# Three pooling chunks move from the input projection into the even attention; a low-rank chunk in stacked parts

## What is computed

```python
# layer 0 (even)
h = rms_norm(x, norm_mix_w[0])
u, q, k, v = split(h @ w_in)                 # 512 | 512 | 128 | 128 columns
# pooling: 4 groups of 128 channels, trailing windows 2/4/8/16
total = csum[:, base:base + l, lo:hi] - csum[:, base - w:base - w + l, lo:hi]
diff = total / count - ext[:, POOL_STATE:, lo:hi]
outs.append(einsum('blc,cd->bld', diff, w_pool[g]))
ya = concatenate(outs) * scale
yb = sliding_window_attention(rope(q), rope(k), v, sinks)   # 8 heads on 2 KV heads, own chunk + 2 before
x = x + concatenate([ya, yb]) @ w_out
x = x + conv_ffn(rms_norm(x, norm_ffn_w[0]))
# layer 1 (odd): the input projection has, among others, a low-rank part of 16 columns
cq, ck, cv, cg, cr, dq, dk, dvv = split(h @ w_in)
log_a = log_sigmoid(cr @ w_gate2 + b_gate) / GATE_NORM      # forget gate of the linear attention
```

## Time and profile before

| | us |
|---|---|
| median of three runs | 1280.73 |
| the profiled execution | 1279.63 |
| its span, first to last instruction | 1277.5 |
| even layer: input projection | about 10 to 81 |
| even attention with output chunks | 81 to 154 |
| even second output pass | 154 to 178 |
| odd layer: input projection begins | 577 |

### The profile page before, as it was taken

The page is one execution under the profiler, slowest core; times in us unless marked ns, Lnnn a source line. Parts: engine busy times, 40 slices in busy tenths (PEclk is TensorE's granted clock), DMA queues, the critical chain, the costliest instruction groups (busy, mean ns, idle before and its releaser), DMA issues.

```text
span 1277.5 us, 24157 instructions
## 1 busy us (share of the span) xinstructions
PE 1223.4 (96%) x9325; PEld 1178.8 (92%) x9325; DVE 807.4 (63%) x1206; ACT 261.8 (20%) x514; POOL 699.6 (55%) x565
## 2 busy tenths in 40 slices
PE   6978899999999999999999998899999999999995
PEld 6967799999999999999999986799999999999995
DVE  6987577778787731126534688766777777762222
ACT  3015332111111200002111165422111111110002
POOL 6732257655665666665653441256665566566661
PEclk9989999999999999999999999999999999999998
DMA  5311123222222223223222310132222222222221
GB/s 212 116 58 34 32 71 100 82 82 96 85 82 86 94 83 100 99 94 115 84 83 67 102 50 33 34 110 85 97 82 82 89 92 82 83 98 93 90 81 71
DMA packets 35522, 108.88 MB, mean 85 GB/s; under 512 B 5984, under 2 KB 7792, under 8 KB 35472
## 3 DMA queue, kind: packets, MB, share of 16 engines
q1 hardware_dynamic: 29232, 102.51, 24.0%
q10 hardware_dynamic: 6240, 5.64, 1.4%
HBM read 103.00 MB, written 5.13 MB: 85 GB/s over the span
## 4 chain that ended last, share of the span: by engine, by line
PE 87%; DVE 9%; ACT 2%; issue 1%; DMA 0%; POOL 0%; ACTq 0%; POOLq 0%; SPq 0%; DVEq 0%
PE psum L424 21%; PE psum L426 20%; PE psum L425 20%; PE psum L437 6%; PE psum L435 4%; PE psum L436 4%; PE psum L438 4%; PE psum L439 3%; DVE even_winsum L1358 1%; PE psum L754 1%; PE psum L621 1%; DVE small L1579 1%; DVE even_rope_swapped L1340 1%; ACT diff_probs L1091 0%; DVE even_diff L1361 0%
## 5 line engine op out<-in xcount | busy, mean ns | idle before, releaser
L424 PE MATMUL psum<-h_hi,w_hi 128*128 128x272 f32 x2032 | 593.7, 292 | 14.4 <-DVE h_lo L1190 10.3
L426 PE MATMUL psum<-h_hi,w_lo 128*128 128x272 f32 x2032 | 588.8, 290 | 0.0
L425 PE MATMUL psum<-h_lo,w_hi 128*128 128x272 f32 x2032 | 585.8, 288 | 0.0
L395 POOL TENSOR_TENSOR w_lo<-w_raw,w_hi 128x1024 fp32r<-128x1024 f32 x187 | 465.1, 2487 | 15.6
L424 PEld LDWEIGHTS psum<-h_hi,w_hi 128*128 128x128 f32 x2032 | 383.2, 189 | 19.6 <-issue 16.7
L425 PEld LDWEIGHTS psum<-h_lo,w_hi 128*128 128x128 f32 x2032 | 383.9, 189 | 0.2
L426 PEld LDWEIGHTS psum<-h_hi,w_lo 128*128 128x128 f32 x2032 | 383.1, 189 | 0.0
L392 POOL TENSOR_TENSOR tick<-tick 1x1 f32<-1x1 f32 x183 | 38.5, 210 | 523.7 <-PE psum L426 444.4
L393 POOL TENSOR_SCALAR w_hi<-w_raw 128x1024 fp32r<-128x1024 f32 x187 | 197.5, 1056 | 9.3 <-DMA w_raw<-in_weights 8.0
L437 PE MATMUL psum<-y_both,w_hi 128*128 128x480 f32 x352 | 133.4, 379 | 0.0
L1290 DVE TENSOR_TENSOR x<-x,psum 128x240 f32 (+1 forms) x16 | 6.4, 401 | 176.1 <-PE psum L439 176.0
(11 more groups left out here) (217 smaller groups left out, 1456.1 us busy)
## 6 DMA issues: line engine op xcount, KB each, us to landing
w_raw<-in_weights SPq DMA_DIRECT2D x187, 512.0 KB, 3.5
x<-in_x SPq DMA_DIRECT2D x8, 272.0 KB, 5.6
out_y<-x SPq DMA_DIRECT2D x8, 272.0 KB, 2.4
out_diff_v_new<-odd_dv ACTq DMA_DIRECT2D x1, 1024.0 KB, 6.2
out_diff_k_new<-odd_kT ACTq DMA_DIRECT2D x1, 1024.0 KB, 4.7
even_rope<-in_rope ACTq DMA_DIRECT2D x1, 544.0 KB, 3.9
odd_rope<-in_rope ACTq DMA_DIRECT2D x1, 544.0 KB, 3.6
consts<-in_consts ACTq DMA_DIRECT2D x1, 384.5 KB, 4.7
```

The source lines that it names most:

```text
L395: pool.tensor_tensor(w_lo[:, k], w_raw[:, k % RAW], w_hi[:, k].bitcast(F32), ALU.subtract).then_inc(w_ready, 1)
L424: pe.matmul(out, wh, xh[:, cols], start=first and n == 0, stop=False)
L425: pe.matmul(out, wh, xl[:, cols], start=False, stop=False)
L426: ins = pe.matmul(out, wl, xh[:, cols], start=False, stop=last and n == len(pairs) - 1)
```

## The change

- The input projection of the even layer has 7 chunks: v, k, two of q, pooling group 3, two of q. v is transposed after the seventh. Scores of unit 0 are issued after the sixth chunk.
- The other three pooling chunks (`pool_fill`) are cut into steps of one to eight slices and put between the parts of the attention units, by the table `EVEN_U`; they use accumulator 3 and each waits for the evacuation of the one before. Window sums and differences are cut up too (`pool_add`, `pool_diff`) and stand between DVE's attention work.
- Pooling products are made half by half in bank 5 (`pool_product`, table `EVEN_POOL`); ACT scales each half into `even_diff` and makes the high part, DVE the low part from SBUF (`pooled_low`).
- The values of all blocks go to bank 4; bank 5 is free for the products.
- Output chunks 0 and 1 are cut up in the attention by `EVEN_OUT`; chunks 2 to 7 follow it and rotate over accumulators 0, 1 (the scores' banks) and 3.
- Maxima and normalisation of a unit are one group instead of two, with the sinks negated once; ACT's small exponential is one instead of two. ACT takes the exponentials of unit u + 2 ahead of the evacuation of unit u + 1. The five DMA issues for the new k and v stand after the exponentials of unit 2.
- `out_norm` makes all eight normalised slices within the pass in both layers.
- The high part of the attention half and its low part have places of their own (`e_hi`, `e_lo`), and so have `probs` and `probsT`, since h must live through the attention.
- The low-rank chunk has its 16 columns twice, at 0 to 15 and 32 to 47; POOL copies the low weights over the second set of the high ones, and PE issues 32 matmuls of 48 output rows instead of 48 (`low_rank`). The gate weights are stacked likewise, 48 rows. DVE works the first gate half at n = 2 and the second at n = 3.

The diff, cut to its core:

```diff
+        POOL_ORDER = [3, 2, 1, 0]
+
+
+
+        EVEN_U = {(-1, 1): (1, 0, 8), (0, 0): (2, 0, 1), (0, 1): (2, 1, 3), (1, 0): (2, 3, 4), (1, 1): (2, 4, 6),
+                  (2, 0): (2, 6, 8), (2, 1): (3, 0, 1), (3, 0): (3, 1, 2), (3, 1): (3, 2, 4), (4, 0): (3, 4, 5),
+                  (4, 1): (3, 5, 7), (5, 0): (3, 7, 8)}
+        EVEN_POOL = {(1, 1): (0, 0), (2, 0): (0, 1), (3, 0): (1, 0), (3, 1): (1, 1), (5, 0): (2, 0), (5, 1): (2, 1),
+                     (6, 1): (3, 0), (7, 0): (3, 1)}
+        EVEN_OUT = {(5, 1): (0, 0, 2), (6, 1): (0, 2, 3), (8, 0): (0, 3, 4), (9, 0): (1, 0, 2), (9, 1): (1, 2, 4)}
+
+        def pooled_acc(m):
+
+            return 3 if m < 2 else (0, 1, 3)[(m - 2) % 3]
...
+            pool.wait_ge(w_ready, S_ODD_IN + 1)
+            cr = S_ODD_IN % RING
+            pool.tensor_scalar(w_hi[:, cr].rearrange("p (c m) -> p c m", c=KC)[:, :, 32:48],
+                               w_lo[:, cr].bitcast(F32).rearrange("p (c m) -> p c m", c=KC)[:, :, 0:16],
+                               1.0, 0.0, ALU.mult, ALU.add).then_inc(stacked, 1)
...
+            def low_rank(acc, s, c):
+
+                wh = w_hi[:, s % RING, c * P:c * P + 48]
+                for half in range(2):
+                    cols = slice(half * HALF, (half + 1) * HALF)
+                    out = psum[0:48, 2 * acc + half, 0:HALF]
+                    pe.matmul(out, wh, h_hi[:, c, cols], start=c == 0, stop=False)
+                    ins = pe.matmul(out, wh, h_lo[:, c, cols], start=False, stop=c == KC - 1)
+                return ins
...
-                    if n >= (2 if n_norm else 3):
+                    if n_norm and n >= 2:
                         pe.wait_ge(evac, ev0 + n - 1)
+                    if not n_norm and n == 3:
+                        pe.wait_ge(rms_ready, 1)
+                    if not n_norm and n >= 4:
+                        pe.wait_ge(evac, (1, 2, 5)[n - 4])
+                    if n_norm and n == 0:
+                        pe.wait_ge(stacked, 1)
...
+                if n == EVEN_PROJ - 2:
+                    even_scores(0)
+                if n == EVEN_PROJ - 1:
+                    pe.wait_ge(evac, 3)
...
+            def pool_fill(i, k0, k1):
+                s = EVEN_PROJ + i - 1
+                if k0 == 0:
+                    pe.wait_ge(w_ready, s + 1)
+                    pe.wait_ge(evac, EVEN_PROJ + i - 1 if i > 1 else EVEN_PROJ - 1)
+                ins = tiles(3, s, h_tiles(k0, k1), k0 == 0, k1 == KC)
+                if k1 == KC:
+                    ins.then_inc(slab_done, 1)
...
+            def pool_product(i, half):
+
+                if half == 0:
+                    pe.wait_ge(diff_ready, i + 1)
+                if i == half == 0:
+                    pe.wait_ge(in_even, 16 * NEVEN)
+                    pe.wait_ge(evac, EVEN_PROJ)
                 else:
-                    pe.wait_ge(evac, ev)
-                out_chunk(s_out + m // 2, m, 3, y_hi, y_lo, 0)
-
-
-            even_scores(0)
+                    pe.wait_ge(pool_out, 2 * i + half)
+                g = POOL_ORDER[i]
+                pe.matmul(psum[:, 5, 0:HALF], e_wpool[:, g], e_diff[:, g, half * HALF:(half + 1) * HALF],
+                          start=True, stop=True).then_inc(pool_mm, 1)
...
+            def pooled_fill(m, i0, i1):
+                s = S_EVEN_OUT + m // 2
+                if i0 == 0:
+                    pe.wait_ge(w_ready, s + 1)
+                    if m == 0:
+                        pe.wait_ge(evac, EVEN_IN)
+                    elif m == 1:
+                        pe.wait_ge(x_upd, 1)
+                    elif m >= 4:
+                        pe.wait_ge(x_upd, m - 2)
+                for i in range(i0, i1):
+                    if m == 0:
+                        pe.wait_ge(pool_lo, i + 1)
+                    c = POOL_ORDER[i]
+                    ins = tiles(pooled_acc(m), s, [(4 * (m % 2) + c, y_hi[:, c], y_lo[:, c])], i == 0, i == 3)
+                if i1 == 4:
+                    ins.then_inc(slab_done if m % 2 else mid_done, 1)
...
+            in_projection(0, 0, 0, EVEN_PROJ, even_side)
+            even_fill(-1, 1)
             even_scores(1)
-            pe.wait_ge(evac, EVEN_IN)
-            pool_product(0, 3)
             for u, (b, c) in enumerate(EU):
                 (q0, nq), _, runs = even_block(b)
-                pe.wait_ge(p_norm, 2 * u + 2)
+                pe.wait_ge(p_norm, u + 1)
                 pr = probs[u % 2][:, :].rearrange("p (h k) -> p h k", h=4)
                 for kb, (_, kn) in enumerate(runs):
                     for j in range(4):
                         ins = pe.transpose(psum[0:kn, 2 * (u % 2) + kb, j * nq:(j + 1) * nq],
                                            pr[0:nq, j, kb * P:kb * P + kn], ident[0:nq, 0:nq])
                 ins.then_inc(p_turned, 1)
-                if u in EVEN_FILL:
-                    out_fill(S_EVEN_OUT, EVEN_FILL[u], 0, EVEN_IN)
                 if u >= 1:
                     even_values(u - 1)
+                even_fill(u, 0)
                 if u + 2 < len(EU):
                     even_scores(u + 2)
+                even_fill(u, 1)
             even_values(9)
-            for m in range(len(EVEN_FILL), KC):
-                out_fill(S_EVEN_OUT, m, 0, EVEN_IN)
-            pe.wait_ge(y_lo_done, 9)
+            for m in range(2, KC):
+                pooled_fill(m, 0, 4)
...
+            ac.wait_ge(turned, 1)
+            ac.activation(e_v[:, 0:4], psum[:, 2, :].rearrange("p (t f) -> p t f", t=4), ACT.Copy)
+            ac.activation(e_v[0:SMP, 4], psum[0:SMP, 3, 0:P], ACT.Copy).then_inc(v_out, 1)
+
+            def pooled(i, half):
+
+                g = POOL_ORDER[i]
+                ac.wait_ge(pool_mm, 2 * i + half + 1)
+                ac.activation(e_diff[:, g, half * HALF:(half + 1) * HALF], psum[:, 5, 0:HALF], ACT.Copy,
+                              scale=const("pool_scale")[:, g:g + 1]).then_inc(pool_out, 1)
+                if half:
+                    ac.wait_ge(pool_out, 2 * i + 2)
+                    ac.activation(y_hi[:, g], e_diff[:, g], ACT.Copy).then_inc(pool_hi, 1)
...
             even_exp(0)
-            pooled(4, 0, 3)
+            even_turned(0)
             even_exp(1)
-            even_turned(0)
             for u, (b, c) in enumerate(EU):
-                if u + 1 < len(EU):
-                    even_turned(u + 1)
+                if u >= 1:
+                    even_turned(u)
+                if c == 0 and b >= 1:
+                    even_out(b - 1)
+                if (u, 0) in EVEN_POOL:
+                    pooled(*EVEN_POOL[u, 0])
                 if u + 2 < len(EU):
                     even_exp(u + 2)
-                if c == 1:
-                    (q0, nq), _, _ = even_block(b)
-                    ac.wait_ge(o_ready, u + 1)
-                    ac.activation(h_hi[:, 4:8, q0:q0 + nq],
-                                  psum[:, 4 + b % 2, 0:4 * nq].rearrange("p (j q) -> p j q", j=4),
-                                  ACT.Copy).then_inc(y_hi_done, 1)
+                if (u, 1) in EVEN_POOL:
+                    pooled(*EVEN_POOL[u, 1])
+                if u == 0:
+                    dma(io["swa_v_new"][0], e_v[:, 3], out_done)
+                    dma(io["swa_v_new"][1, 0:P - SMP], e_vc[SMP:P, :], out_done)
+                    dma(io["swa_v_new"][1, P - SMP:P], e_v[0:SMP, 4], out_done)
+                    ac.wait_ge(rope_done, 1)
+                    dma(io["swa_k_new"][:, 0], e_kT[:, SEQ - P:SEQ], out_done)
+                    dma(io["swa_k_new"][:, 1], e_kT[:, KEYS - P:KEYS], out_done)
+            even_out(4)
...
+            for n in range(4):
+                even_in(n)
+            pool_in(0)
             even_max(0)
+            even_in(5)
+            even_normalise(0)
+            even_in(6)
+            for i in (1, 2):
+                pool_add(3, i)
+            pool_in(1)
             even_max(1)
-            pooled_low(4, 0, 3)
-            even_normalise(0)
             for u, (b, c) in enumerate(EU):
                 if u + 1 < len(EU):
                     even_normalise(u + 1)
-                if u in EVEN_FILL:
-                    out_first(S_EVEN_OUT, EVEN_FILL[u], 0, 0)
                 if c == 0 and b >= 1:
                     even_low(b - 1)
+                if u == 2:
+                    pool_in(2)
+                if u == 5:
+                    pool_in(3)
+                if u == 7:
+                    pooled_low(2)
                 if u + 2 < len(EU):
                     even_max(u + 2)
-            for m in range(len(EVEN_FILL), KC):
-                out_first(S_EVEN_OUT, m, 0, 0)
-            even_low(4)
+                if u == 0:
+                    for i in (3, 4):
+                        pool_add(3, i)
+                    pool_diff(3)
+                if u == 1:
+                    for i in (1, 2, 3):
+                        pool_add(2, i)
+                if u == 2:
+                    pool_diff(2)
+                if u == 3:
```

(21 more changed lines are left out.)

288 lines of the change are left out of this document (129 added, 159 removed).

## The result

The changed kernel takes **1283.68 us** (median of 18 runs, 1281.66 to 1285.87), the kernel before, in runs beside it, 1280.37 us (18 runs, 1279.58 to 1282.07). The ratio is 1.0024 (95% interval 1.0017 to 1.0031): slower by 3.1 us by the ratio (3.3 by the medians), just over the 0.2% that a measurement of this kernel can tell from no change. The forecast was 1281.4 us, no change. The profiled execution spans 1281.9 us against 1277.5.

The account below looks back on a forecast made before the run. TensorE was taken as the bound, busy 1223.4 of 1277.5 us. Even part +1.6, odd part -1.0 and norms +0.1 gave +0.7 us, 1280.3 for the profiled execution and 1281.4 us as median; range 1278.5 to 1284, with rivals 1274.5 to 1287.

Parts of the forecast that it names:

- (a): Early even attention: PE waits for DVE's pooling evacuation before the third pooling chunk, with two POOL meetings; 4.1 us idle.
- (b): Before unit 3's scores: PE waits for ACT's evacuation of unit 1's transposes, behind exponentials and five DMA issues; 3.7 us idle.
- (c): Units 3 to 7 and before unit 8: ACT's order makes a 5.1 us loop between scores; 4.7 us idle.
- (d): Output chunk 0's third step waits for the third pooled remainder, behind unit 8's normalisation on DVE; 4.7 us idle.
- (e): The last two attention units of the even layer: 2.3 us idle.
- three episodes: Low clock after three long even-part stalls: 1.54 us each plus half a microsecond for slow scores; 5.1 us against 5.7.
- The products in halves: Even-layer pooling products made in halves are not dearer: 0 to -0.8 us, taken as -0.5.
- The odd projection: Low-rank chunk gains 0.6 us, its last step awaiting the last slice; gate split removes a 0.43 us wait; -1.0 us.
- The norms: All normalised slices inside the second output pass: DVE's added instructions cost 0, at most 0.1 us.
- The cover: First of three rivals: even-part window sums precede POOL's split, only one stall draws the low clock; 1275.6 us, chance 0.27.
- the third rival: PE's idle time between 56 and 155 us merely moves, leaving the odd part's gain; 1279.7 us, chance 0.05.
- The low clock on the chain: Second of three rivals: even-part scores after stalls run at half clock, adding 5.5 us; 1286.9 us, chance 0.28.

Follow-up runs that it names:

- e6: Changed kernel with its odd-layer part undone (48 full matmuls, no stacked copy, gate work unsplit); 1287.33 us, ratio 1.0049 to the kernel before.
- e9: Kernel before with 25 unread matmuls added at the start of the even layer's second output pass; 1283.78 us, ratio 1.0024.
- e10: e5 with ACT's evacuations ahead at units 1 and 6, unit 8's maxima and the third pooled remainder earlier on DVE; 1273.60 us.
- e5: Changed kernel with four edits: DMA issues late, second pooling evacuation first, last rotation first, third pooled remainder early; 1271.09 us, ratio 0.9930.
- e2: Changed kernel with DVE taking the second pooling chunk's evacuation and unit 1's maxima ahead of the first two window sums; 1282.17 us, ratio 1.0014.
- e3: Changed kernel with DVE rotating the last query chunk before normalising unit 0; 1280.45 us, ratio 1.0003 to the kernel before.
- e12: e10 with DVE taking the third pooling chunk's evacuation ahead of unit 3's normalisation; 1272.17 us, ratio 0.9934 to the kernel before.
- e8: e5 with ACT evacuating every unit's transposes ahead of the next unit's exponentials; 1289.82 us, ratio 1.0073 to the kernel before.

## Why the prediction was right or wrong

**The number.** 1281.4 us was forecast, with a range of 1278.5 to 1284; 1283.7 lies at its upper end. The direction was not forecast: no change was expected, and the kernel is 3.1 us slower. Of the signs named, the gap before the second pooling chunk of the attention (3.02 us), the one in output chunk 0 (4.55), the start of the pass (157.51) and the odd layer's total came as said. The gap before unit 3's scores was 1.88 us, not 3 to 4.5, and PE waited 0.35 us within the first seven chunks.

**The added idle: right in all, off in its parts.** Forecast 19.5 us, measured 19.1. That the sum is so close is luck in part: (a) came out 1.4 us over its forecast and (b) 1.8 under. (a) 4.1 forecast, 2.50 + 3.02 = 5.5 measured: the step had the last rotation done at 64.4, in time for unit 1's scores. It came at 66.5, since the last step of it met POOL's split, which began when the second pooling chunk ended, and the normalisation ahead of it had met the split before that one. I had counted two meetings with POOL behind 63.9 us, both on the window sums. (b) 3.7 forecast, 1.9 measured: the chain was as long as counted (10.3 us from the maxima of unit 1 at 70.77 to the scores at 81.06, the five issues 1.5 of it and not 2.1), but PE, at the low clock, was busy for 8.2 us of it where I had 6.3. (c) 4.7 and 5.2 (1.1, 0.9, 0 and 3.1): the meeting that made the last one so long (one small instruction of unit 7's maxima took 1.43 us instead of 0.16, held up by POOL's split of the slab that the fourth pooling chunk frees) wasn't in my sum. (d) 4.7 and 4.6. (e) 2.3 and 2.0. The seven chunks, priced at nothing, cost 0.35 us.

**The clock in the even part: right in size, blind to its spread.** I took 5.1 us for three episodes. In after's timeline the groups that ran slow (unit 2's scores 1.05 us over, the matmuls around them 0.7, 0.4 and 0.9, a pooling product 0.5, unit 2's transposes 0.3, the step behind 124.36 and unit 7's transposes 0.7 each) add up to 5.2. But e6, with the same code there, had 2.9 us more, with the same waits behind 124 us. So 5.1 us is one draw of several that executions make, not a fixed price.

**The products in halves: wrong or hidden.** I counted -0.5 us for them. The even part is longer by 3.2 us, of which 2.3 are idle time and 0.35 the first chunks; the clock by these rows gives -0.5. That leaves 1.1 us of busy time, 1.6 over a sum with the products' -0.5, for which no run names an instruction. The rows allow an estimate. The number of matmuls is the same, but when the three-part matmuls follow another kind, the second starts 0.20 to 0.23 us behind the first instead of 0.127; from 9 us to the pass this happens 13 times in before and 19 times in after, about 0.6 us. And half a product takes 0.36 to 0.66 us to the next start (0.52 in the mean of five in after, so 1.04 for two), where the one whole product of before with work right behind it, at 64.24, takes 0.72: up to 1.3 us for four. By this the -0.5 had the wrong sign. No run takes either alone, so it stays an estimate.

**The odd projection: right.** -1.0 forecast, -1.13 measured, with both terms (0.6 and 0.43; 0.66 and 0.47) and the reason for the first: the last slice, not PE's work, ends the chunk. **The norms:** right, the second pass is followed by a stretch as full as before.

**What the sum lacked: a term for the odd attention.** I let every change of the even part arrive at the end as it is. After's trace has the low stretch in the odd attention that before's does not have, and after's median has 1.2 us of it by the groups of the runs: 1280.4 + 3.2 - 1.1 + 1.2 = 1283.7. Why the changed kernel has it more often stays open. These 1.2 us and the 1.6 us of the even part above, less the 0.4 us by which the kernel before was faster than in its first three runs, are in the main what separates 1281.4 from 1283.7.

**The rivals.** The cover didn't hold: PE idle 19.1 us, not under 14. That idle time merely moves (the third rival) is nearer: 2.3 us were added, not none. The low clock on the chain is half true: unit 2's scores, six matmuls behind the stall of 3.0 us, ran slow, but the scores directly behind the stalls before units 1, 3, 5, 6 and 8 did not, and the clock from 64 to 135 us was 0.88 (0.90 before), over the 0.85 from which I let it decide. Its price was near: unit 2's scores lost 1.05 us. The first rival took before's clock to fall at fixed places, since three runs lay within 1.7 us; 17 runs beside e9 spread over 3.8.

**The lock.** In the meetings shown here, DVE's instruction ends behind POOL's: 3.25 us from 81.64 with POOL's end at 83.81 in e10, 2.26 us for 4 elements in e5. The Trainium skill, SBUF — State Buffer, section "SBUF: two separate sides", calls it an exclusive lock for a whole instruction, and adds that DVE takes part with two inputs from SBUF, against a POOL instruction that reads SBUF. By this, the trace agrees: in after a reduce that reads PSUM alone takes its usual 1.23 us inside POOL's subtraction, and the instruction behind it, with two inputs from SBUF, takes 0.70 us instead of 0.16 and ends 0.02 us behind POOL's:

```profile
90.66 2.38 POOL L415 TENSOR_TENSOR w_lo<-w_raw,w_hi 128x1024 fp32r<-128x1024 f32 x1
91.10 1.23 DVE L1463 TENSOR_REDUCE small<-psum 128x4 f32<-128x1024 f32 x1 [0.91 <-PE psum L613]
92.36 0.70 DVE L1465 SCALAR_TENSOR_TENSOR small<-small,neg_sinks 128x4 f32<-128x4 f32 x1
```

## What to carry to other kernels

When fill work is woven into a chain, go through each engine's queue and ask of every instruction what stands ahead of it that waits for another engine: here one remainder behind a normalisation cost 5.2 us, one rotation 2.7, five DMA issues 1.5 on the chain, and the order without them is 0.7% faster than the kernel before. A single edit's price is easily hidden: e2 and e3 still led by 3.4 and 4.0 us at output chunk 0 and lost most of it to the low clock behind, and in e12 the gap moved to the next wait. An order that helps at one engine can lose 18 us when the others keep theirs (e8). A sum to a microsecond is no use where the low clock draws its 1 to 3 us anew in each execution; compare the lowest runs and the positions of equal work in the traces, not medians alone.
